# Router products that read rows in front of their layer norm, with the norm's gain and bias worked into the router matrix

## The reference

```python
h = _layer_norm(ALPHA * h + mix, *norms[i][0])
h = _layer_norm(ALPHA * h + _hier_moe(h, *moes[i]), *norms[i][1])
...
# _layer_norm(z, g, b): (z - mean) * rsqrt(var + LN_EPS) * g + b
# _hier_moe starts with its router:
coarse = xf @ w_coarse + b_coarse                 # 4 groups
fine_all = einsum('td,gde->tge', xf, w_fine) + b_fine   # 4 x 8 experts
# then the best group, its two best experts, their gates; rows are sorted by expert
```

## Time and profile before

| | us |
|---|---|
| median of 3 runs | 2509.14 (2507.9 to 2513.69) |
| the profiled execution: its own time | 2510.11 |
| its span | 2508.4 |
| PE busy | 2261.5 (90%) |
| DVE busy | 824.3 (33%) |
| ACT busy | 481.3 (19%) |
| POOL busy | 310.3 (12%) |

### The profile page before, as it was taken

The page is one execution under the profiler, slowest core; times in us unless marked ns, Lnnn a source line. Parts: engine busy times, 40 slices in busy tenths (PEclk is TensorE's granted clock), DMA queues, the critical chain, the costliest instruction groups (busy, mean ns, idle before and its releaser), DMA issues. The chain is left out here.

```text
span 2508.4 us, 33396 instructions
## 1 busy us (share of the span) xinstructions
PE 2261.5 (90%) x13415; PEld 1280.6 (51%) x13415; DVE 824.3 (33%) x1599; ACT 481.3 (19%) x890; POOL 310.3 (12%) x265
## 2 busy tenths in 40 slices
PE   5999978789958999999976999999985999999994
PEld 4687545554545445555533555554454544554551
DVE  5652025554242101111116466664324111111116
ACT  2222124341110000000003344442110000000001
POOL 5243000001101101111102000001100110111102
PEclk9999987889968999999988999999986999999997
DMA  4100010002229999999959211102108999999967
GB/s 149 36 19 17 17 69 1 1 1 72 67 83 382 420 421 391 419 418 386 421 202 311 87 38 38 38 19 56 58 40 317 419 420 403 417 416 420 387 287 288
DMA packets 144328, 529.81 MB, mean 211 GB/s; under 512 B 40002, under 2 KB 63074, under 8 KB 127792
## 3 DMA queue, kind: packets, MB, share of 16 engines
q1 hardware_dynamic: 122640, 490.93, 49.3%
q0 software_dynamic: 13600, 33.84, 3.5%
q10 hardware_dynamic: 7936, 2.90, 0.5%
HBM read 500.50 MB, written 40.50 MB: 216 GB/s over the span
## 5 line engine op out<-in xcount | busy, mean ns | idle before, releaser
L1721 PE MATMUL l_main_pgu<-l_w_ring,l_ex_xT 128*64 128x256 f32 (+1 forms) x4992 | 484.9, 383 | 1.7 <-DVE l_ex_xT L1796 1.7
L1721 PEld LDWEIGHTS l_main_pgu<-l_w_ring,l_ex_xT 128*64 128x64 f32 (+1 forms) x4992 | 292.8, 129 | 183.4 <-issue 41.1
L1767 PE MATMUL l_main_py<-l_w_ring,l_ex_hT 128*64 128x512 f32 (+1 forms) x1248 | 239.3, 595 | 1.6 <-DVE l_ex_hT L1838 1.6
L1718 PE MATMUL l_main_pgu<-l_w_ring,l_ex_xT 128*128 128x512 f32 x384 | 174.4, 609 | 7.9 <-DMA l_w_ring<-in_l_moe_w_gate 7.9
L1838 DVE COPY l_ex_hT<-l_main_ph 128x256 f32<-128x256 f32 (+1 forms) x78 | 36.3, 465 | 385.1 <-PE l_main_ph L1742 385.1
L2179 PE MATMUL lru_pr<-h2T,lru_wz 128*128 128x352 f32 (+1 forms) x480 | 144.4, 462 | 11.8 <-ACTq L2234 11.8
L1834 DVE TENSOR_TENSOR l_ex_hid<-l_ex_sil,l_main_pgu 128x256 f32<-128x256 f32 (+1 forms) x78 | 36.0, 462 | 350.8 <-PE l_main_pgu L1721 269.3
L2197 PE MATMUL lru_pg<-h2T,lru_wz 128*128 128x512 f32 x320 | 148.7, 592 | 0.0
L1767 PEld LDWEIGHTS l_main_py<-l_w_ring,l_ex_hT 128*64 128x64 f32 (+1 forms) x1248 | 71.5, 128 | 136.6 <-issue 129.6
L2179 PEld LDWEIGHTS lru_pr<-h2T,lru_wz 128*128 128x128 f32 x480 | 92.7, 193 | 64.6 <-ACTq L2234 12.2
L1718 PEld LDWEIGHTS l_main_pgu<-l_w_ring,l_ex_xT 128*128 128x128 f32 x384 | 73.0, 194 | 98.0 <-issue 87.8
(11 more groups left out here) (432 smaller groups left out, 2828.0 us busy)
## 6 DMA issues: line engine op xcount, KB each, us to landing
l_w_ring<-in_l_moe_w_gate SPq DMA_DIRECT2D x64, 2048.0 KB, 23.7
l_w_ring<-in_l_moe_w_up SPq DMA_DIRECT2D x64, 2048.0 KB, 24.9
l_w_ring<-in_l_moe_w_down SPq DMA_DIRECT2D x64, 2048.0 KB, 27.8
l_y<-expert_rows SPq DMA_DIRECT2D x32, 512.0 KB, 8.2
h_rows<-H SPq DMA_DIRECT2D x24, 512.0 KB, 5.4
lru_wz<-in_l_w_in SPq DMA_DIRECT2D x20, 512.0 KB, 4.9
H<-h_rows SPq DMA_DIRECT2D x16, 512.0 KB, 9.6
w_in<-in_l_w_in SPq DMA_DIRECT2D x3, 2048.0 KB, 8.2
```

The lines of the kernel that those rows point to most:

```text
L1718: last = pe.matmul(out[:], x[:, k, :], w[0][:, k, :], start=k == 0, stop=k == KD - 1)
L1721: last = pe.matmul(out[HALF * h + o:HALF * h + o + m, 0:256], x[:, k, it.at + o:it.at + o + m], w[n][:, k, 256 * h:256 * h + 256], start=k ...
L1767: last = pe.matmul(py[b][HALF * h + o:HALF * h + o + m, :], hT[:, c % 2, HALF * (c // 2) + o:HALF * (c // 2) + o + m], ws[n][:, c, 512 * h ...
```

## The change

- The router reads z, the rows in front of the norm, not h. `turn(j)` waits only for the sums (`z_done`); in return, DVE's in-place norm (L950) of tile j waits until tile j is turned. Turned rows go to `zT`.
- The router matrix times the gain (`wg`, `router_weights`) is made once per layer by DVE, and the bias vector spread over 128 columns (`bias_cols`). PE makes, once, the sums over rows of `wg` (with a matrix of ones) and of bias times `wr` (`router_sums`), in front of the first `router`. The logits of a tile are then `r * product + (-mean * r * sums + offset)`, three small DVE operations (`nm`, `shift`, logits).
- PE's loop becomes output(j, 0), turn(j-1), output(j, 1), router(j-1), and then turn(n-1), router(n-1). There are two PSUM tiles `pl`.
- ACT copies the turned tile ahead of the same tile's square root and scale.
- Gain and bias are loaded a second time as columns (`ln_cols`, pieces of 4 bytes, 2 DMAs of 1024 pieces); in layer 0 all nine router loads are issued by ACT at the start, in layer 1 by SP as before.
- In layer 0 DVE makes `wg` and `bias_cols` behind the statistics of tile 0, and the route constants behind those of tile 1. In layer 1 it makes all of them ahead of the first tile's sums.
- The wait for the stores of h is moved from the end of the projection to the end of SP's part in `route`.

```diff
+        if read:
+            dve.wait_ge(*read)
...
+        self.stored = nc.alloc_semaphore(f"{L}_h1_stored")
+        K.h1_stored = self.stored, 16 * self.n
...
+        if self.first:
+            self.load_router(sp)
...
-        sp.wait_ge(self.stored, 16 * self.n)
...
+    def load_router(self, eng):
...
+            for c, x in enumerate(("g", "b")):
+                eng.dma_start(self.ln_cols[:, c, :], A[f"{L}_ln1_{x}"].rearrange("(k p) -> p k", p=P)).then_inc(self.r_loaded, 16)
...
         def turn(j):
             m = TILES[first + j][1]
-            pe.wait_ge(self.norm.h_ready, j + 1)
+            pe.wait_ge(self.z_done, 2 * (j + 1))
+            if self.short(j):
+                pe.wait_ge(self.norm.var_ready, j + 1)
+            if j:
+                pe.wait_ge(self.zT_ready, 2 * j)
             for k in range(KD):
                 last = pe.transpose(pt[k // 4][:, k % 4, 0:m], K.H[0:m, first + j, P * k:P * k + P], K.ident[0:m, 0:m])
             last.then_inc(self.turned, 1)
+        def router_sums():
+            pe.wait_ge(self.consts, 14)
+            pe.wait_ge(self.r_loaded, 9 * 16)
+            pe.wait_ge(self.wg_ready, 2)
+            for k in range(KD):
+                pe.matmul(pl[1][:, 0:36], K.route_constants.ones[:], self.wg[:, k, :], start=k == 0, stop=k == KD - 1)
+            for k in range(KD):
+                last = pe.matmul(pl[1][:, 64:100], self.bias_cols[:, k, :], self.wr[:, k, :], start=k == 0, stop=k == KD - 1)
+            last.then_inc(self.sums_ready, 1)
...
         def router(j):
             m = TILES[first + j][1]
             if j == 0:
-                pe.wait_ge(self.r_loaded, 7 * 16)
-            pe.wait_ge(self.hT_ready, 2 * (j + 1))
+                router_sums()
+            pe.wait_ge(self.zT_ready, 2 * (j + 1))
             if j >= 1:
-                pe.wait_ge(self.lg_done, j)
+                pe.wait_ge(self.lg_done, max(j - 1, 1))
             for k in range(KD):
-                last = pe.matmul(pl[0:m, 0:36], self.hT[:, k, 0:m], self.wr[:, k, :], start=k == 0, stop=k == KD - 1)
+                last = pe.matmul(pl[j % 2][0:m, 0:36], self.zT[:, k, 0:m], self.wg[:, k, :], start=k == 0, stop=k == KD - 1)
...
-        for j in range(n + 3):
-            if j < n:
-                if j >= 2:
-                    pe.wait_ge(self.z_done, 2 * (j - 1))
-                if self.short(j):
-                    short_output(j)
-                else:
-                    output(j, 0)
-            if j >= 3:
-                router(j - 3)
-            if j < n and not self.short(j):
+        for j in range(n):
+            if j >= 2:
+                pe.wait_ge(self.z_done, 2 * (j - 1))
+            if self.short(j):
+                short_output(j)
+            else:
+                output(j, 0)
+            if j >= 1:
+                turn(j - 1)
+            if not self.short(j):
                 output(j, 1)
-            if 2 <= j < n + 2:
-                turn(j - 2)
+            if j >= 1:
+                router(j - 1)
+        turn(n - 1)
+        router(n - 1)
...
+        if not self.first:
+            self.load_router(act)
+        for j in range(self.n):
+            m = TILES[self.first + j][1]
+            act.wait_ge(self.turned, j + 1)
+            act.wait_ge(self.lg_ready, j)
+            for h in range(2):
+                act.copy(self.zT[:, 4 * h:4 * h + 4, 0:m], self.pt[h][:, :, 0:m]).then_inc(self.zT_ready, 1)
+            self.norm.scalar(act, self.first + j)
...
+        def router_weights():
+            dve.wait_ge(self.r_loaded, 9 * 16)
+            dve.tensor_tensor(self.wg[:], self.wr[:], bc(self.ln_cols[:, 0, :], 36), ALU.mult).then_inc(self.wg_ready, 1)
+            dve.tensor_copy(self.bias_cols[:], bc(self.ln_cols[:, 1, :], P)).then_inc(self.wg_ready, 1)
+        def logits(j):
+            i = first + j
+            m, rs = TILES[i][1], norm.rs[:, i % 2:i % 2 + 1]
+            if j == 0:
+                dve.wait_ge(self.sums_ready, 1)
+                do(dve.tensor_copy(self.col_sum[:], self.pl[1][:, 0:36]), wait=False)
+                do(dve.tensor_tensor(self.offset[:], self.pl[1][:, 64:100], self.rb[:], ALU.add))
+            do(dve.scalar_tensor_tensor(out=self.shift[0:m, :], in0=self.col_sum[0:m, :], scalar=self.nm[0:m, :], in1=self.offset[0:m, :], op0=ALU.mult, op1=ALU.add))
+            dve.wait_ge(self.lg_ready, j + 1)
+            dve.scalar_tensor_tensor(out=K.logits[0:m, i, :], in0=self.pl[j % 2][0:m, 0:36], scalar=rs[0:m, :], in1=self.shift[0:m, :],
+                                     op0=ALU.mult, op1=ALU.add).then_inc(self.lg_done, 1)
+            dve.wait_ge(self.lg_done, j + 1)
+        if first:
+            K.route_constants.dve(dve, do, self.consts)
+            router_weights()
+        for j in range(n):
+            rows(j)
+            if j:
+                logits(j - 1)
+            norm.vector(dve, do, first + j, (self.turned, j + 1))
+            b, m = (first + j) % 2, TILES[first + j][1]
+            dve.wait_ge(norm.scales_ready, j + 1)
+            do(dve.tensor_scalar(self.nm[0:m, :], norm.mv[0:m, 0:1], norm.rs[0:m, b:b + 1], -1.0, ALU.mult, ALU.mult))
+            if j == 0 and not first:
+                router_weights()
+            if j == 1 and not first:
+                K.route_constants.dve(dve, do, self.consts)
+        logits(n - 1)
...
+            sp.wait_ge(*K.h1_stored)
```

More of the change, by code:

```diff
@@ L1035, in sync @@
             store(j)
-        sp.wait_ge(self.stored, 16 * self.n)
+    def load_router(self, eng):
+        A, L, wr, rb = self.A, f"l{self.layer}", self.wr, self.rb
+        with self.nc.allow_non_contiguous_dma(reason="router weights"):
+            eng.dma_start(wr[:, :, 0:GROUPS], A[L + "_moe_w_coarse"].rearrange("(k p) g -> p k g", p=P)).then_inc(self.r_loaded, 16)
+            for g in range(GROUPS):
+                c = GROUPS + PER_GROUP * g
+                eng.dma_start(wr[:, :, c:c + PER_GROUP], A[L + "_moe_w_fine"][g].rearrange("(k p) e -> p k e", p=P)).then_inc(self.r_loaded, 16)
+            eng.dma_start(rb[:, 0:GROUPS], A[L + "_moe_b_coarse"].rearrange("(a g) -> a g", a=1).to_broadcast([P, GROUPS])).then_inc(self.r_loaded, 16)
+            eng.dma_start(rb[:, GROUPS:36], A[L + "_moe_b_fine"].rearrange("(a g) e -> a (g e)", a=1).to_broadcast([P, NE])).then_inc(self.r_loaded, 16)
+            for c, x in enumerate(("g", "b")):
+                eng.dma_start(self.ln_cols[:, c, :], A[f"{L}_ln1_{x}"].rearrange("(k p) -> p k", p=P)).then_inc(self.r_loaded, 16)
     def tensor(self, pe, last_slice=None):
@@ L1145, in vector, with rows @@
-        dve.wait_ge(self.lg_done, n)
+        def rows(j):
+            i = first + j
+            m = TILES[i][1]
+            dve.wait_ge(self.res_loaded[j % 2], 16 * (j // 2 + 1))
+            for g in range(4 if self.short(j) else 0):
+                c = slice(256 * g, 256 * g + 256)
+                dve.wait_ge(self.o_ready, 2 * j + 2)
+                ins = dve.scalar_tensor_tensor(out=K.H[0:m, i, c], in0=self.res[j % 2][0:m, c], scalar=ALPHA, in1=self.po[j % 2][0][32 * g:32 * g + m, 0:256],
+                                               op0=ALU.mult, op1=ALU.add)
+                if g < 2:
+                    do(ins, wait=False)
+                else:
+                    ins.then_inc(self.z_done, 1)
+            for h in range(0 if self.short(j) else 2):
+                c = slice(512 * h, 512 * h + 512)
+                dve.wait_ge(self.o_ready, 2 * j + h + 1)
+                dve.scalar_tensor_tensor(out=K.H[0:m, i, c], in0=self.res[j % 2][0:m, c], scalar=ALPHA, in1=self.po[j % 2][h][0:m, :],
+                                         op0=ALU.mult, op1=ALU.add).then_inc(self.z_done, 1)
+            dve.wait_ge(self.z_done, 2 * j + 2)
+            do.wait()
```

63 lines of the change are left out of this document (11 added, 52 removed).

## The result

The changed kernel takes 2490.51 us (median of 6 runs, 2486.47 to 2494.5) against 2509.22 us (6 runs) of the kernel before: ratio 0.9926, 95% interval 0.9914 to 0.9938, so 15.6 to 21.6 us less. Forecast were 2486.5 us and the range 2481 to 2495. The profiled execution took 2486.47 us with a span of 2483.9 and a mean granted clock of 0.95 (before: 2508.4 and 0.941).

The account below looks back on a forecast made before the run. No engine is full: a dependent chain bounds each projection's end, PE the stretch ahead. Layer 0's -13.1 and layer 1's -9.5 give -22.6 from 2510.11: 2487.5, with the median 1.0 lower 2486.5 us; range 2481 to 2495.

Parts of the forecast that it names:

- The tail: End of each layer's projection, last residual sum's start to last logits' end: 7.0 us, gaining 15.3 and 15.2 us.
- T: Start of a layer's last residual sum; forecast to move by +2.2 us in layer 0, +5.7 in layer 1.
- The hole: PE's wait for route constants at the first logits disappears, giving back 4.63 us in layer 0, 1.15 in layer 1.
- The sums' price: Sums over matrix and bias times matrix on PE: 16 matmuls at steady price, 3.40 us per layer.
- (a): Layer 1's preparation on DVE, 5.9 to 8.1 us, fits its 13.44 us idling, costing nothing.
- (b): Layer 0's loads and preparation ready at 588.2, just before PE wants them; counted 0, bounds 0 to 2.5 us.
- (c) and (d): Layer 0's constants behind tile 1 on DVE, 4.2 to 6.4 us; in-place norm and reordered copies; all at no cost.
- (e): Wait for the stores, moved into `route`: costs nothing, SP's last store having all of `route` to land.
- (1): Router loads land late in layer 0, PE waits at the sums; 2489 to 2494 us; chance 0.16.
- (2): Router loads land so late that PE loses 12 to 22 us (chance 0.05) or the kernel is slower (0.03).
- (3): Last product or DVE's queue keeps the tail's chain; 2488 to 2490 us; chance 0.70 together with the forecast.
- (4): DVE's small operations overlap, PE stays at 2.4 GHz into `route`; 2 to 5 us more gained; chance 0.06.

Follow-up runs that it names:

- first repeat: The changed kernel run and profiled again with no edit; 2491.59 us.
- experiment 4: The kernel before, with only the route constants moved to the start of DVE's part of the projection, in both layers; 2501.54 us, ratio 0.9956.
- Experiments 1 and 2: The changed kernel with the sums cut to 2 matmuls a layer (2511.27 us), and with all 16 spread two by two between wide matmuls (2487.91 us).
- second repeat: The changed kernel run and profiled once more with no edit; 2494.58 us.
- experiment 3: The changed kernel with layer 0's nine router loads issued by SP in place of ACT; 2489.81 us.
- mixed version: The changed kernel with the sums' 16 matmuls spread two by two between the wide matmuls of output(2, 0), router(0) behind; 2487.91 us, ratio 0.9899.

## Why the prediction held, and the term that was off

**The tail** was right in mechanism and price: 7.23 and 7.14 us for 7.0, 7.14 to 7.73 in the repeats. Each step up to the last product is there: PE goes on to router(n-2) at T - 0.2, statistics start at T + 2.08 (forecast 2.1), the norm's first operation at T + 3.7. The last product went the other way. I had argued that the clock stays up, since PE idles for only 1.1 us in front of it, and had set "below 2 us" as a sign. It idled for 1.16 and took 3.13 us in layer 0 and 2.60 in layer 1, and the granted clock of the tail's window is 0.80, so that step failed. It cost next to nothing, because DVE's chain is as long. Where the product was slow from its start it is no longer hidden, as in layer 0 of the first repeat (3.63 us, DVE waits, tail 7.73; the prediction's 7.65 for this case):

```profile
713.88 0.26 DVE L1183 SCALAR_TENSOR_TENSOR logits<-l_pl,l_ln_rec_dev,l_shift 128x36 f32<-128x36 f32 x1 [0.62 <-PE l_pl L1106]
```

The 0.2 that is missing of the forecast: the small operations take 0.21 to 0.26 us in place of 0.20, and start 0.25 to 0.38 apart. Gains 15.04 and 15.02 for 15.3 and 15.2.

**The hole** was right: experiment 4 measured it by itself, 4.7 us from the phase's start and 1.3, for 4.63 and 1.15.

**The sums' price was the mis-sized term.** I put 16 matmuls at 3.40 us a layer, all "at its steady prices". Experiments 1 and 2 confirm that price: 14 matmuls gone give 3.0 to 3.1 beside the clock. In executions without a fall T moved by 131.89 - 129.56 = 2.33 and 126.07 - 120.09 = 5.98 us, against +2.2 and +5.7 forecast. What the sum lacked is the clock behind the row. Over the three profiles of the changed kernel it costs (1.6 + 0 + 1.7) / 3 = 1.1 us in layer 0 and (3.4 + 1.7 + 3.3) / 3 = 2.8 in layer 1. So the term is 4.5 and 6.2 us, not 3.4 and 3.4. The forecast's -22.6, plus 3.9 for the clock, 0.4 for T and 0.4 for the tails, is -17.9; measured were -18.7, with -15.6 to -21.6 as the interval. That the median of 2490.51 lies 4.0 above the forecast of 2486.5 is thus, within what the runs tell, the clock's 3.9. That the profiled execution's 2486.47 us stands so near to the 2487.5 that the sum gives for it is luck: it lost 5.0 us to the clock behind the sums and won 7.8 outside the projections, which its repeats did not. I had asked of the clock only where PE idles: in the hole, and in front of the tail's last product. That it can fall with PE busy was not in the sum, in the range or among the rivals.

**The covers.** (a) held in full. DVE made the constants and the matrix from 1703.56 to 1708.9, then idled:

```profile
1707.86 0.46 DVE L1170 TENSOR_TENSOR l_w_router_gain<-l_w_router,l_ln_cols 128x288 f32<-128x288 f32 x1
...
1708.24 0.69 DVE L1171 COPY l_ln_bias_cols<-l_ln_cols 128x1024 f32<-128x1024 f32 x1
...
1716.92 1.48 DVE L1163 SCALAR_TENSOR_TENSOR H<-l_res,lru_pr 128x512 f32<-128x512 f32 x2 [8.00 <-PE lru_pr L1059]
```

5.4 us of work (forecast 5.9 to 8.1) and 8.00 us of idling behind it. (b) held with next to nothing to spare. DVE's timeline in layer 0:

```profile
583.70 0.46 DVE L1170 TENSOR_TENSOR l_w_router_gain<-l_w_router,l_ln_cols 128x288 f32<-128x288 f32 x1 [1.05 <-DMA l_ln_cols<-in_l_ln_b]
583.76 2.60 POOL L979 TENSOR_TENSOR H<-H,l_ln_bias 16x1024 f32<-16x1024 f32 x1 [12.03 <-ACT H L971]
584.07 2.84 DVE L1171 COPY l_ln_bias_cols<-l_ln_cols 128x1024 f32<-128x1024 f32 x1
```

The last loads landed at 583.70, the copy ran beside POOL's bias sum and took 2.84 us in place of 0.69 (the price in layer 1), and it was done at 586.91, 0.86 ahead of the first sum on PE, which had no wait. In the second repeat 0.15 us were left (done at 588.75, sums at 588.90). The meeting with POOL that I had bounded at 2.5 us happened, at 2.84 - 0.69 = 2.2. What paid for it was not ACT's early start but the landing, 583.70 - 569.52 = 14.2 us after the phase's first load (14.3 and 15.4 in the repeats) and 14.7 in experiment 3 on SP, for 586.5 - 570.7 = 15.8 in my sum, and PE, which came to the sums 18.25 us after that load and not 17.7.

(c) and (d) left no wait on PE. (e), the moved wait for the stores, cost nothing and was worth something, though the prediction gives it no value and no experiment tests it. The last store is issued at 713.38 and lands after 2.6 us, at 716.0, 1.9 behind the last logits; in layer 1 it lands at 1855.4, again 1.9 behind them. Before, it landed at 711.8, long ahead of the last logits at 726.4. As an estimate from these rows, with the wait left where it was, each tail would have given back some 1.9 us less.

**Rivals.** (1), a new wait at the sums, and (2), its unbounded form: no idle time stands in front of L1093 in any profile. In time the result, 2490.51, lies just above my own range (2484 to 2490) and inside (1)'s (2489 to 2494), so the number alone would have spoken for (1); the rows speak against it. (3) named a longer tail and the lower clock, with 2488 to 2490: the size fits, and the clock was the lower one for part of the tails, but they are only 0.4 us over the forecast together, and the loss lies behind the sums. (4): PE's clock is higher in the tail's window than before (0.80 for 0.61), but it fell within it all the same, and the chain there was DVE's.

## What to carry to other kernels

Small products on a PE that bounds the stage cost 0.11 us a record at the upper clock here, whether they have 36 columns or 72, and a long row of them can cost PE's clock behind it as well, in wide products that were full before. Join them (more columns on the moving side were free up to 72 here) before spreading them; here that gave back 1.8 us of price and 0 to 3.4 of clock a layer, and no version was faster than its 2481.85 us. A chain at a phase's end is worth rewriting in algebra: moving the norm's scale behind the product took 15 us off each tail. But 3.4 us of that was work that only moved ahead, and the sums cost 3.4 us and the clock behind them up to 3.4 more, so that the two projections together gained 17 to 20 us. And look for what ends next: here the landing of the last store would have, 1.9 us later.

## What the hardware showed that I had not expected

- PE's granted clock falls to 1.2 GHz with PE busy in every slice: the 48 records of 36 columns of layer 1 were followed by 0.50 in 1726.0 to 1731.5, and rows that begin with the 32 of the sums by a loss in 7 of 10 places; the same program has it in one execution and not in the next. The Trainium skill ("TensorE: Matmul & The Clock Gate", section "Why this matters for your kernels") names idle gaps between bursts of matmuls as what takes the clock down; here it fell without one.
- At the lower clock the 36-column products cost 3.61 us for 16 records in place of 1.87, so their price goes with the clock although it doesn't go with their columns.
- A DVE copy with one input took 2.84 us beside POOL's bias sum and 0.69 without it; the multiplication in experiment 3 took 2.20 in place of 0.46 in the same way. Both ended 0.3 to 0.6 us after POOL's operation. In the mixed version, where POOL's operation started 0.3 us after the copy had, the two took 0.46 and 0.69.
- Nine router loads had landed 14.7 us after the phase's start when SP issued them, and 14.2, 14.3 and 15.4 when ACT did: the issuing engine makes no difference that these runs show. PE came to the sums at 18.26 and 18.25 us either way.
